# Another order for an RWKV recurrence, its block transfers on ScalarE's queue, and one attention head's scores in float32

## The reference

```python
q = rope(rms_norm(a_q...), positions); k = rope(rms_norm(a_k...), positions)
s = einsum('bqhd,bqnhd->bqhn', qb, kg) * att_scale      # over the selected keys
p = softmax(where(sel_ok, s, -inf)); out = einsum('bqhn,bqnhd->bqhd', p, vg)
```

```python
def step(state, inp):
    r_t, w_t, k_t, v_t, kk_t, a_t = inp
    sa = einsum('bhvk,bhk->bhv', state, -kk_t)
    state = state * w_t + sa[..., None] * (kk_t * a_t) + v_t[..., None] * k_t
    return state, einsum('bhvk,bhk->bhv', state, r_t)
```

## Time and profile before

| | |
|---|---|
| median of 3 runs | 3493.98 us (3491.92 to 3501.32) |
| profiled execution, its own time | 3500.6 us |
| its span, first to last instruction | 3498.8 us |
| mean granted PE clock | 0.984 of full speed |
| busy: PE, DVE, ACT, POOL | 3364.9, 1818.4, 1408.5, 415.1 us (96, 52, 40, 12%) |

### The profile page before, as it was taken

How to read it: one execution, slowest core, us unless ns; L and a number is a source line. 1 busy time by engine, 2 the same in 40 slices (tenths; PEclk the granted TensorE clock), 3 DMA queues, 4 the chain that set the end, 5 groups by cost and what they waited for, 6 DMA issues and landing times.

```text
span 3498.8 us, 51676 instructions
## 1 busy us (share of the span) xinstructions
PE 3364.9 (96%) x21012; PEld 2673.5 (76%) x21012; DVE 1818.4 (52%) x2380; ACT 1408.5 (40%) x1616; POOL 415.1 (12%) x718
## 2 busy tenths in 40 slices
PE   7899999999999999999999999999999988999897
PEld 1566888888887788888887867888888866777785
DVE  5745666666667333444423457242424247777445
ACT  1323344344434223444423236141414167777423
POOL 0000222322122000000000000000000023444000
PEclk9999999999999999999999999999999999999898
DMA  9522232333233442222222313333333333332321
GB/s 351 184 73 80 98 102 90 108 102 102 99 104 102 139 145 85 84 84 84 84 90 90 132 62 134 124 122 121 120 120 120 134 93 83 71 88 61 126 97 72
DMA packets 178956, 381.46 MB, mean 109 GB/s; under 512 B 111728, under 2 KB 117104, under 8 KB 145008
## 3 DMA queue, kind: packets, MB, share of 16 engines
q1 hardware_dynamic: 164352, 326.73, 28.3%
q0 software_dynamic: 14448, 52.50, 4.4%
HBM read 342.49 MB, written 35.13 MB: 108 GB/s over the span
## 4 chain that ended last, share of the span: by engine, by line
PE 85%; DVE 4%; DMA 3%; POOLq 3%; SPq 2%; issue 1%; ACT 1%; DVEq 1%; POOL 0%; ACTq 0%
PE PJ L294 18%; PE PJ L296 18%; PE PJ L295 18%; PE AB L294 6%; PE AB L296 6%; PE AB L295 6%; POOLq L1582 1%; POOLq L1579 1%; PE AB L233 1%; DMA WK<-ada 1%; PE AB L681 1%; DMA X<-blocks_scratch 1%; PE AB L1677 1%; PE AB L1686 1%; PE AB L447 1%
## 5 line engine op out<-in xcount | busy, mean ns | idle before, releaser
L294 PE MATMUL PJ<-XH,WH 128*128 128x512 f32 x2848 | 1127.5, 396 | 17.2 <-DVE XL L421 10.3
L296 PE MATMUL PJ<-XH,WL 128*128 128x512 f32 x2848 | 1111.7, 390 | 0.0
L295 PE MATMUL PJ<-XL,WH 128*128 128x512 f32 x2848 | 1110.9, 390 | 0.0
L325 DVE TENSOR_TENSOR WL<-RAW,WH 128x2048 fp32r<-128x2048 f32 (+2 forms) x239 | 543.1, 2273 | 695.3 <-ACT WH L320 691.4
L320 ACT ACTIVATE WH<-RAW 128x2048 fp32r<-128x2048 f32 (+2 forms) x240 | 453.6, 1890 | 914.9 <-PE PJ L296 655.0
L294 PEld LDWEIGHTS PJ<-XH,WH 128*128 128x128 f32 x2848 | 536.2, 188 | 142.4 <-issue 29.7
L296 PEld LDWEIGHTS PJ<-XH,WL 128*128 128x128 f32 x2848 | 535.9, 188 | 113.3
L295 PEld LDWEIGHTS PJ<-XL,WH 128*128 128x128 f32 x2848 | 536.4, 188 | 109.6 <-issue 1.9
L294 PE MATMUL AB<-XH,WH 128*128 128x512 f32 (+1 forms) x960 | 380.9, 397 | 10.0 <-DVE XL L421 7.7
L295 PE MATMUL AB<-XL,WH 128*128 128x512 f32 (+1 forms) x960 | 375.0, 391 | 0.0
L296 PE MATMUL AB<-XH,WL 128*128 128x512 f32 (+1 forms) x960 | 375.0, 391 | 0.0
(11 more groups left out here) (448 smaller groups left out, 3880.5 us busy)
## 6 DMA issues: line engine op xcount, KB each, us to landing
RAW<-w SPq DMA_DIRECT2D x232, 1024.0 KB, 4.9
WK<-ada SPq DMA_DIRECT2D x32, 1024.0 KB, 6.5
GATE<-gate POOLq DMA_DIRECT2D x64, 256.0 KB, 3.1
rkvg_scratch<-WK POOLq DMA_DIRECT2D x16, 1024.0 KB, 4.7
x_scratch<-X POOLq DMA_DIRECT2D x8, 1024.0 KB, 5.9
X<-rkvg_scratch SPq DMA_DIRECT2D x32, 256.0 KB, 3.7
RAW<-rkvg_scratch SPq DMA_DIRECT2D x32, 256.0 KB, 3.5
X<-xT SPq DMA_DIRECT2D x4, 1024.0 KB, 15.8
```

The lines of the kernel that those rows point to most:

```text
L294: nc.tensor.matmul(bank[0:width, n, :], hi, xh, start=first, stop=False)
L295: nc.tensor.matmul(bank[0:width, n, :], hi, xl, start=False, stop=False)
L296: m = nc.tensor.matmul(bank[0:width, n, :], lo, xh, start=False, stop=last)
L325: nc.vector.tensor_tensor(WL[k % 2][:, :, 0:w], narrow(RAW[k % 2], w), WH[k % 2][:, :, 0:w].bitcast(F32), ALU.subtract).then_inc(wl_ready, 1)
```

## The change

First, the last attention head takes its scores from the unsplit query and key, in full float32, one matmul for each block in place of three; its high copy on ACT and low difference on DVE go. Second, the turns of the recurrence are written in another order on all five engines: the hops of a pair are all in one turn, steps have other lags and places, `dve_reff` is a step of its own, and several waits change with it. Third, `sp_blocks_out` becomes `blocks_out(eng, q)`, and from pair 1 on it is ACT that issues its two DMAs, right behind its copy of the same blocks. What is computed stays the same but for the rounding of the one head's scores. The diff, where the turns are cut to what the listings below don't show:

```diff
+        def is_last(h):
+
+            return isinstance(h, int) and h == HEADS - 1
+
...
             elif k == 2:
+                if is_last(h):
+                    pe.wait_ge(s("at_roped"), 2 * h + 1)
+                    for b in range(TB):
+                        m = nc.tensor.matmul(AB[:, b, 0:ROW_W[b]], wk(4)[:, b * P:(b + 1) * P], wk(5)[:, 0:ROW_W[b]],
+                                             start=True, stop=True)
+                    m.then_inc(s("at_scores"), 1)
+                    return
...
             elif k == 2:
-                wait(act, s("at_roped"), 2 * h + 1)
-                nc.scalar.activation(AT_HI, wk(4, 2), ACT.Copy).then_inc(s("at_sd"), 1)
+                if not is_last(h):
+                    wait(act, s("at_roped"), 2 * h + 1)
+                    nc.scalar.activation(AT_HI, wk(4, 2), ACT.Copy).then_inc(s("at_sd"), 1)
                 wait(act, s("at_masked"), h + 1)
...
             elif k == 2:
-                wait(dve, s("at_sd"), 2 * h + 2)
-                nc.vector.tensor_tensor(AT_LO, wk(4, 2), AT_HI.bitcast(F32), ALU.subtract).then_inc(s("at_roped"), 1)
+                if not is_last(h):
+                    wait(dve, s("at_sd"), 2 * h + 2)
+                    nc.vector.tensor_tensor(AT_LO, wk(4, 2), AT_HI.bitcast(F32), ALU.subtract).then_inc(s("at_roped"), 1)
...
-        def sp_blocks_out(sp, q):
-
-            sp.wait_ge(wv("nt_sb"), q + 1)
+        def blocks_out(eng, q):
+
+            eng.wait_ge(wv("nt_sb"), q + 1)
             for r in range(2):
-                sp.dma_start(by_row(n_d[q % 2], r), ws(N_OF(q))[rows(r)].rearrange("p (z i) -> p z i", i=CH)
+                eng.dma_start(by_row(n_d[q % 2], r), ws(N_OF(q))[rows(r)].rearrange("p (z i) -> p z i", i=CH)
                              ).then_inc(wv("n_out"), 16)
 
...
         def wv_sp(sp, t):
-            at(t + 1, lambda q: sp_solved_out(sp, q), 1)
-            at(t + 2, lambda q: sp_blocks_out(sp, q), 2)
-            at(t + 3, lambda q: sp_load_lora(sp, q), 3)
+            at(t + 3, lambda q: sp_load(sp, q), 3)
             at(t + 1, lambda q: sp_solved_back(sp, q), 1)
             at(t + 2, lambda q: sp_blocks_in(sp, q), 2)
+            at(t + 3, lambda q: sp_load_lora(sp, q), 3)
             at(t + 2, lambda q: sp_levels(sp, q), 2)
-            at(t + 4, lambda q: sp_load(sp, q), 4)
+            at(t + 2, lambda q: sp_solved_out(sp, q), 2)
+
 
...
         def pe_lora(pe, q):
             pe.wait_ge(wv(f"lw_in{q % 2}"), 16 * (q // 2 + 1))
             wait(pe, wv("masked"), 3 * q - 2)
+            wait(pe, wv("oa_sb"), q - 2)
             nc.tensor.matmul(bank(2), LW2(q)[:, 0:P], TW[0:LORA, :], start=True, stop=True)
...
         def pe_token_d(pe, q):
-            pe.wait_ge(wv("factors"), 4 * q + 1)
+            pe.wait_ge(wv("factors"), 4 * q + (2 if q else 1))
             if q:
                 pe.wait_ge(wv("tok_sb"), token_copied(q, 2))
-                pe.wait_ge(wv("keys"), key_logged(min(q + 1, PAIRS - 1)))
             pe_token(pe, T_D, token_bank(q, 0))
 
...
         def pe_nt(pe, q):
             pe.wait_ge(wv("factors"), 4 * q + 2)
-            wait(pe, wv("oa_sb"), q - 1)
             pe_pairs(pe, q, T_D, 2, wv("nt"))
 
...
         def pe_pq(pe, t, f):
-            if f == 1:
+            if f == 0:
                 pe.wait_ge(wv("inverse"), 3 * t + 3)
-            else:
                 pe.wait_ge(wv("bv"), min(t + 2, PAIRS))
             for m in (2 * f, 2 * f + 1):
...
         def pe_fg(pe, t):
+            pe.wait_ge(wv("pq_sb"), t + 1)
             pe.wait_ge(wv("masked"), 3 * min(t + 2, PAIRS))
             for m in range(TB):
...
         def pe_oa(pe, t):
-            pe.wait_ge(wv("pq_sb"), t + 1)
+            pe.wait_ge(wv("masked"), 3 * min(t + 2, PAIRS - 1) + 1)
             k = kept(t)
...
         def act_gate(act, q):
+            wait(act, wv("gs"), q)
             A(ws(T_SG), ws(T_IN(q) + T_G), ACT.Sigmoid).then_inc(wv("keys"), 1)
 
```

More of the change, by code:

```diff
@@ L1805, in wv_pe @@
             at(t + 1, lambda p: pe_hop(pe, p, 2))
-            at(t + 3, lambda p: pe_token_d(pe, p), 1)
             at(t + 1, lambda p: pe_hop(pe, p, 3))
-            at(t + 4, lambda p: pe_lora(pe, p), 2)
-            at(t + 1, lambda p: pe_hop(pe, p, 4))
+            at(t + 3, lambda p: pe_token_k(pe, p), 1)
+            at(t + 1, lambda p: pe_hop(pe, p, 4))
+            at(t + 4, lambda p: pe_ss(pe, p), 2)
+            at(t + 1, lambda p: pe_hop(pe, p, 5))
+            at(t + 2, lambda p: pe_level_w(pe, p, 0))
+            at(t + 1, lambda p: pe_hop(pe, p, 6))
+            at(t + 3, lambda p: pe_token_e(pe, p), 1)
+            at(t + 1, lambda p: pe_hop(pe, p, 7))
+            at(t + 2, lambda p: pe_level_y(pe, p, 0))
+            at(t + 4, lambda p: pe_lora(pe, p), 2)
+            at(t + 3, lambda p: pe_bonus(pe, p), 1)
+            at(t + 2, lambda p: pe_level_w(pe, p, 1))
+            at(t + 3, lambda p: pe_bt(pe, p))
+            at(t + 2, lambda p: pe_level_y(pe, p, 1))
+            at(t + 4, lambda p: pe_token_v(pe, p), 1)
         A = nc.scalar.activation
@@ L1934, in wv_act @@
         def wv_act(act, t):
+            at(t + 1, lambda p: act_r1(act, p))
+            at(t + 3, lambda p: act_key_square(act, p), 2)
+            at(t + 3, lambda p: act_key(act, p), 2)
+            at(t + 2, lambda p: act_token(act, p, 1), 1)
+            at(t + 3, lambda p: act_key_log(act, p), 2)
+            at(t + 1, lambda p: act_level(act, p, 0))
+            at(t, lambda p: act_oa(act, p))
+            at(t + 2, lambda p: act_token(act, p, 3), 1)
+            at(t + 3, lambda p: act_key_norm(act, p), 2)
@@ L1935, in wv_act @@
+            at(t + 3, lambda p: act_sig_decay(act, p), 2)
+            at(t + 3, lambda p: act_sig_rate(act, p), 2)
             at(t + 1, lambda p: act_level(act, p, 1))
-            at(t + 3, lambda p: act_sig_decay(act, p), 2)
-            at(t + 2, lambda p: act_chunk_decay(act, p), 1)
+            at(t + 3, lambda p: act_decay(act, p), 2)
+            at(t + 3, lambda p: act_rate(act, p), 1)
+            at(t + 3, lambda p: act_decay_before(act, p), 1)
             at(t, lambda p: act_out_square(act, p))
-            at(t + 3, lambda p: act_rate(act, p), 1)
+            at(t + 3, lambda p: act_growth(act, p), 1)
@@ L2033, in dve_level_x, with dve_reff @@
             nc.vector.transpose(ws(T_X), YT(v)).then_inc(wv("inverse"), 1)
+        def dve_reff(dve, t):
+            dve.wait_ge(wv("products"), 2 * t + 1)
+            V(by_parity(ws(T_REFF)), by_parity(ws(RR_OF(t))), quarter(6, CH), ALU.subtract)
         def dve_factors(dve, t):
@@ L2102, in wv_dve @@
         def wv_dve(dve, t):
-            at(t + 2, lambda p: dve_gate(dve, p))
-            at(t + 3, lambda p: dve_sums(dve, p), 2)
-            at(t + 3, lambda p: dve_rate_key(dve, p), 1)
-            at(t + 3, lambda p: dve_sums_before(dve, p), 2)
-            at(t + 3, lambda p: dve_d(dve, p), 1)
-            at(t + 3, lambda p: dve_rr(dve, p), 1)
-            at(t + 3, lambda p: dve_k(dve, p), 1)
+            at(t + 1, lambda p: dve_level_y(dve, p, 0))
+            at(t + 1, lambda p: dve_level_x(dve, p))
+            at(t + 3, lambda p: dve_key(dve, p), 1)
+            at(t + 2, lambda p: dve_bv(dve, p))
+            at(t + 3, lambda p: dve_sums(dve, p), 2)
+            at(t + 2, lambda p: dve_ke(dve, p))
+            at(t + 3, lambda p: dve_sums_before(dve, p), 2)
+            at(t + 1, lambda p: dve_level_y(dve, p, 1))
+            at(t + 3, lambda p: dve_rr(dve, p), 1)
+            at(t + 3, lambda p: dve_rate_key(dve, p), 1)
+            at(t + 3, lambda p: dve_k(dve, p), 1)
+            at(t + 3, lambda p: dve_d(dve, p), 1)
+            at(t + 3, lambda p: dve_k2(dve, p), 1)
+            at(t + 2, lambda p: dve_re(dve, p))
+            at(t - 1, lambda p: dve_result(dve, p))
+            at(t + 2, lambda p: dve_gate(dve, p))
+            at(t + 1, lambda p: dve_reff(dve, p))
+            at(t + 3, lambda p: dve_rd(dve, p), 1)
             at(t + 1, lambda p: dve_factors(dve, p))
-            at(t + 3, lambda p: dve_k2(dve, p), 1)
             at(t + 1, lambda p: dve_gg(dve, p))
-            at(t + 3, lambda p: dve_rd(dve, p), 1)
+            at(t + 3, lambda p: dve_bonus(dve, p), 1)
             at(t + 1, lambda p: dve_hop(dve, p, 1))
@@ L2116, in wv_dve @@
                 dve_split_part(dve, 0)
-            at(t + 3, lambda p: dve_bonus(dve, p), 1)
             at(t + 1, lambda p: dve_hop(dve, p, 2))
+            at(t, lambda p: dve_out_scale(dve, p))
+            at(t + 1, lambda p: dve_hop(dve, p, 3))
             if t == PAIRS - 2:
@@ L2127, in wv_dve @@
                 dve_split_part(dve, 2)
+            at(t + 2, lambda p: dve_inverse(dve, p))
+            at(t, lambda p: dve_out_shift(dve, p))
             at(t + 1, lambda p: dve_hop(dve, p, 5))
-            at(t, lambda p: dve_out_shift(dve, p))
             if t == PAIRS - 2:
@@ L2212, in _ @@
             sp_load_lora(sp, 1)
-            sp_blocks_out(sp, 0)
```

(9 more changed lines are left out.)

75 lines of the change are left out of this document (18 added, 57 removed).

## The result

| | before | after |
|---|---|---|
| median of the runs | 3496.7 us (3491.9 to 3501.3, 4 runs) | 3534.9 us (3530.9 to 3540.8, 4 runs) |
| ratio, 95% interval | | 1.0111 [1.0088, 1.0133] |
| profiled execution's span | 3498.8 us | 3530.6 us |
| first scaled product of the recurrence | 2889.64 | 2883.53 |
| turn, mean of 13 | 25.45 us | 28.83 us |

The change makes the kernel 38 us slower; 3505 was forecast, and 3534.9 lies outside the range. By the two spans (+31.8) the time went thus: -6.1 up to the first scaled product, (28.83 - 25.45) x 13 = +43.9 in thirteen turns, -9.2 in the two behind them, +3.1 after that.

The account below looks back on a forecast made before the run. The prediction took a ring through ACT and PE in the recurrence as closing last: 26.7 against 25.45 us a turn, +16.2 over 13 turns, less 4.9 at the last attention head, +11.3, so 3505 us; range 3484 to 3528.

Parts of the forecast that it names:

- Slower: Whole kernel: slower by over 0.3%, above 3504.5 us, chance 0.45; within 0.38, faster 0.17.
- the ring that closes last: Recurrence: ACT from nt copy through r1 copy, then PE from key transpose through nt; 26.27 us, 26.7 with PE's idling.
- Seven table loads a turn: ACT in the recurrence: seven loads in place of four; three more are 3.9 us a turn.
- two DMAs on ACT: ACT's queue behind the nt copy: issue of the block DMAs taken at 1.31 us a turn.
- ACT busy: ACT in a recurrence turn: 19.8 us rises to 25.0 with three loads and the DMA issue.
- ACT's stretch: ACT from the start of its nt copy to the end of its r1 copy, put at 9.20 us.
- PE's work from key transpose to nt: PE's part of the recurrence turn, run in one piece, put at 16.97 us.
- The head's products: Last attention head on PE: four float32 matmuls put at 2.28 us, the head's gain at 4.9 us.
- the last level's subtraction: DVE in the recurrence: two operations ahead of it make PE's product pq wait, taken at 0.25 us a turn.
- the added waits: Recurrence's new order: costed at nothing, since each names work standing a group or more earlier.
- the slow clock: Rival, chance 0.12: idling at the key transpose slows PE's clock, 1.6 us a turn, 21 us more, 3526.
- the first and last turns: Ends of the recurrence: counted as no different; the last run with a PE clock of 0.64 in either order.

Follow-up runs that it names:

- e3: The kernel after with a one-column dummy Sigmoid on ACT ahead of the pair's two sigmoids, so the table load runs earlier; 3528.8 us.
- e2: The kernel before with only the two block DMAs moved from SP to ACT, right behind its nt copy; 3506.0 us.
- e10: The kernel before with the last attention head's scores in float32 and three dummy matmuls on PE in the recurrence's last two turns; 3482.4 us.
- e1: The kernel before with only the last attention head's scores in float32; 3486.5 us.
- e11: The kernel of e1 once more, run on the same chip as e10 as its partner; 3486.6 us.
- e7: The kernel after with the dummy Sigmoid of e3 and the gate's sigmoid moved behind the other sigmoids and the level copy; 3506.5 us.
- e8: The kernel after with one dummy matmul on PE ahead of each of two waits, the key transpose and the second level's product; 3520.6 us.
- e12: The kernel after with the dummy Sigmoid of e3 and one dummy matmul on PE at the key transpose; 3507.9 us.
- e4: The kernel after with the gate's sigmoid on ACT moved behind the other sigmoids and the level copy, six table loads a turn; 3517.5 us.

## Why the prediction was wrong

**Right.** Slower was the likeliest sign, and the ring that closes last is the one named. Seven table loads a turn, each 1.28 us, two DMAs on ACT of 1.27 us (1.31 taken), ACT busy 167.9 / (205 / 28.83) = 23.6 us a turn (25.0 less the DMAs' 1.3 was the forecast), PE's largest wait at the key transpose for the r1 copy. ACT's stretch was put at 9.20, and that it is in seven of thirteen turns (9.19 to 9.22); the mean is 9.52, by the turns in which the two DMAs took longer to issue. PE's work from key transpose to nt, without the wait, is 17.03 us, with 16.97 and 0.14 of issue forecast. The head's products came at 2.32 for 2.28; up to the recurrence the kernel after gained 6.1 us for 4.9.

**The step that failed** is the sentence that gave "the last level's subtraction" 0.25 us as the only wait inside PE's stretch. In the turn shown pq does not wait at all; the wait in the stretch is 1.23 us, for ACT's level copy, at the level product ahead of that subtraction. In the new order ACT has the two sigmoids of another pair ahead of that copy, and they wait for PE's bonus product. I costed the added waits at nothing because each names earlier work, but left out the one that had moved to the first sigmoid, and did not ask what the moved operations themselves wait for. And I counted the sigmoids' table load as ACT's work, as if it could run beneath the wait, when the wait is on the load. That makes (1.23 - 0.25) x 13 = 12.7 us of the miss, and e3 takes it away by bringing the load forward (1.2 us a turn at full clock). The Trainium skill (ScalarE: Activation LUTs, Step-by-step: what each stage is for) says that the compiler places the load right before its ACTIVATE; the list agrees, and adds that one of the waits may land on the load (1.34 us of idle time ahead of it at 3094.39). A row of the timeline that shows a load at work ahead of a wait (L1841's began at 3087.27, PE's sum was done at 3087.75) says nothing of the next one.

**The second step** is that the slow clock was made a rival (0.12) to the forecast, with a price per turn of its own. It is not another case but a consequence: a ring that makes PE wait 1.1 to 2.6 us at the key transpose lowers the clock in some turns. Turns above the full-clock mean cost (28.83 - 27.8) x 13 = 13 us, some 11 of it by the clock and 2 by the longer issues of the DMAs, where the rival had 21 by the clock, and that came on top of the ring. The reason I gave against it, that 1.4 us is the longest wait in the recurrence, holds only for 2990 to 3195 us. Between 2889 and 2990 us one of 1.9 stands, in turns at 1.00, and in the last turns one of 2.5, and there the clock is down (0.82 in 3220.50 to 3248.44); the same product takes 1.10 us in the earlier trace rows. Waits of PE in 2889 to 2990 us, then its timeline, before:

```profile
PE PJ L1593 <- DMA TBL<-lora: 3.3, 3, 1.9
```

```profile
3227.87 1.98 PE L1677 MATMUL AB<-WS 64*64 64x64 f32 x32 [2.53 <-DVE WS L2023]
```

**The third** is "the first and last turns I count as no different". The last two took 55.7 us and take 46.6, which gave back 9 us. Most of that goes with the clock of the very last turn: 27.8 us at 0.63 before and 21.5 at 0.92 after, while e2 and e10, in the old order, have 21.4 and 22.0 there at 1.00. The time there differs between executions of one kernel (e1 and e11: 50.5 and 53.9 us for the two turns). The turn before it is 2.9 us shorter after (25.0 at 0.86 for 27.9 at 0.82); e7, e8 and e12, at full clock in the new order, need 20.8 to 23.6 for it. How much of this is the order and how much the clock was not tried.

So the sum misses by its parts: +12.7 level wait, +4 ACT's stretch (9.52 for 9.20, times 13), +11 clock, -1 head, -9 last turns, +3 behind them, which is 21 against 31.8 - 11.3 = 20.5 us missed by the spans. The medians differ by 38, 6 more than the spans: before's profiled execution lay 3.9 us above its median (3500.6 to 3496.7), after's 2.6 below (3532.3 to 3534.9).

**Open.** Why e3, with the level wait gone and the others much as they were, ran more turns at a low clock than the kernel after; what at a wait decides whether the clock falls; and why the issue of two DMAs on ACT took 1.27 us in most turns and up to 2.62 in some.

## What to carry to other kernels

Follow a reordered engine's queue operation by operation and ask of each that moved what it waits for and who stands behind it; an operation that needs a new table may take its load behind that wait, and a one-column dummy of the same function brings it forward. A wait of PE inside a loop can have two prices, the wait and the clock behind it; read both from the turns and add them. Before a clock seen in one execution is put down to an edit, look at the granted clock of all executions of both kernels. Where an order leaves one engine with no slack, check the next ring (here the loads, one turn later than before) before promising what a cut is worth.

## What the hardware showed that I had not expected

- In the kernel after, turns whose waits of PE were no longer than 1.23 us ran at 0.94 in some cases and at 1.00 in others: 1.22 us ahead of L1619 stood in both. Two dummy matmuls a turn kept it at 1.00 in twelve turns of twelve (e8).
- The same 1.23 us of wait at L1695, with none at the key transpose, left ten of twelve turns at 1.00 (e4).
- Two DMAs took ACT 1.27 us to issue in most turns and up to 2.62 in some; four of half the size took 2.59 to 3.72. In the mean it is about 0.8 us for each DMA in both.
